# Two output projections: the merged activation's high and low parts side by side, one wide product for both, and two reads of the result

## The reference, cut to what matters

```python
# first block
merged = (gates[:, :, 0] * jnp.einsum('bsc,cd->bsd', ya, w_proj_rnn[l])
          + gates[:, :, 1] * jnp.einsum('bsc,cd->bsd', yb, w_proj_attn[l]))
x = x + jnp.einsum('bsd,de->bse', merged, w_out[l])        # output projection 1
h = rmsnorm(x, norm2_g[l])                                 # then up, gate, down
...
# second block
y = jax.nn.sigmoid(g_a) * (o_a @ w_o_swa[l]) + jax.nn.sigmoid(g_b) * (o_b @ w_o_mla[l])
x = x + y @ w_out[l]                                       # output projection 2
h = rmsnorm_2(x, ffn_norm_g[l])
x = x + (jax.nn.silu(h @ w_gate[l]) * (h @ w_up[l])) @ w_down[l]
```

## Time and profile before

| What | us |
|---|---|
| Median of 3 runs | 799.68 (799.31 to 800.32) |
| The profiled execution | 799.39 |
| Its span, first to last instruction | 797.6 |
| TensorE busy | 790.2 (99%) |
| TensorE weight loads busy | 692.8 (87%) |
| VectorE busy | 583.0 (73%) |
| ScalarE busy | 453.2 (57%) |
| GpSimd busy | 77.1 (10%) |

### The profile page before, as it was taken

How to read it: one execution, slowest core, us unless ns; L and a number is a source line. 1 busy time by engine, 2 the same in 40 slices (tenths; PEclk the granted TensorE clock), 3 DMA queues, 4 the chain that set the end, 5 groups by cost and what they waited for, 6 DMA issues and landing times.

```text
span 797.6 us, 12039 instructions
## 1 busy us (share of the span) xinstructions
PE 790.2 (99%) x4632; PEld 692.8 (87%) x4632; DVE 583.0 (73%) x706; ACT 453.2 (57%) x592; POOL 77.1 (10%) x90
## 2 busy tenths in 40 slices
PE   8999999999999999999999999999999999999997
PEld 8998888888889899999999897888799888888886
DVE  5994899566477888787877877666778766666664
ACT  7669846666435654445354758757455544454444
POOL 2330232000002100000000532410003000000000
PEclk9999999999999999999999999999999999999999
DMA  8744556434545455455454452444345555555521
GB/s 306 255 174 152 203 177 244 160 127 141 207 159 179 158 207 196 163 205 198 171 204 165 166 201 96 159 159 137 140 161 209 196 187 181 187 194 178 207 105 53
DMA packets 22582, 140.88 MB, mean 177 GB/s; under 512 B 3474, under 2 KB 3730, under 8 KB 6546
## 3 DMA queue, kind: packets, MB, share of 16 engines
q1 hardware_dynamic: 22114, 139.77, 49.2%
q10 hardware_dynamic: 432, 0.62, 0.3%
HBM read 139.33 MB, written 1.05 MB: 176 GB/s over the span
## 4 chain that ended last, share of the span: by engine, by line
PE 97%; DMA 1%; SPq 0%; DVE 0%; ACT 0%; issue 0%
PE pp L1566 21%; PE pp L1529 20%; PE pp L1531 20%; PE pp L1530 20%; PE pp L1568 10%; PE pp L1682 1%; DMA raw<-in_slabs 1%; PE pp L1708 1%; PE pp L1695 1%; PE pp L1671 1%; PE pp L1617 0%; PE pp L1745 0%; PE pp L1629 0%; PE pp L1645 0%; PE pp L1637 0%; SPq L466 0%
## 5 line engine op out<-in xcount | busy, mean ns | idle before, releaser
L946 DVE TENSOR_TENSOR wlo<-raw,whi 128x2048 fp32r<-128x2048 f32 x129 | 298.2, 2314 | 100.4 <-ACT whi L514 100.2
L514 ACT ACTIVATE whi<-raw 128x2048 fp32r<-128x2048 f32 x129 | 246.4, 1911 | 97.9 <-PE pp L1531 97.5
L1566 PE MATMUL pp<-ahilo,whi 128*128 128x512 f32 x704 | 221.4, 396 | 0.0
L1529 PE MATMUL pp<-whi,ahi 128*128 128x512 f32 (+2 forms) x412 | 163.0, 396 | 0.0
L1531 PE MATMUL pp<-whi,alo 128*128 128x512 f32 (+2 forms) x412 | 159.5, 387 | 0.0
L1568 PEld LDWEIGHTS pp<-ahilo,wlo 128*128 128x128 f32 x704 | 132.2, 188 | 31.1
L1530 PE MATMUL pp<-wlo,ahi 128*128 128x512 f32 (+2 forms) x412 | 159.2, 386 | 0.0
L1568 PE MATMUL pp<-ahilo,wlo 128*128 128x256 f32 x704 | 138.3, 278 | 0.0
L1529 PE MATMUL pp<-ahi,whi 128*128 128x256 f32 x448 | 127.8, 285 | 1.0 <-DVE wlo L1047 0.6
L1531 PE MATMUL pp<-ahi,wlo 128*128 128x256 f32 x448 | 126.7, 283 | 0.0
L1530 PE MATMUL pp<-alo,whi 128*128 128x256 f32 x448 | 126.7, 283 | 0.0
(11 more groups left out here) (230 smaller groups left out, 755.1 us busy)
## 6 DMA issues: line engine op xcount, KB each, us to landing
raw<-in_slabs SPq DMA_DIRECT2D x125, 1024.0 KB, 4.8
raw<-in_slabs SPq DMA_DIRECT2D x4, 512.0 KB, 8.3
raw<-in_slabs SPq DMA_DIRECT2D x2, 832.0 KB, 5.0
raw<-in_slabs SPq DMA_DIRECT2D x2, 576.0 KB, 3.8
raw<-in_slabs SPq DMA_DIRECT2D x4, 256.0 KB, 5.8
x_res<-in_xT SPq DMA_DIRECT2D x3, 256.0 KB, 6.4
out<-gg SPq DMA_DIRECT2D x3, 256.0 KB, 2.0
gate<-in_final_norm_g SPq DMA_DIRECT2D x1, 512.0 KB, 6.6
```

Source lines behind the costliest of these rows:

```text
L514: e.activation(whi[slot][:, :], raw[slot][:, :], ACT.Copy).then_inc(hi_ready, 1)
L946: e.tensor_tensor(wlo[slot][:, :], raw[slot][:, :], whi[slot][:, :].bitcast(f32), ALU.subtract).then_inc(lo_ready, 1)
L1529: e.matmul(out, lhs[0], rhs[0], start=first, stop=False, skip_group_check=True)
L1566: e.matmul(out[:, m, :], w[m][0], ACT2[:, k, :], start=k == 0, stop=False, skip_group_check=True)
```

## The change

The merged activation gets the side-by-side layout (`ACT0`), the projection slabs use `feature_pairs` on it, each slab writes a pair of banks (pair 1 for its first and third slab, pair 0 for its second and fourth), and VectorE adds first the left halves of both banks to the residual, then the right halves.

```diff
+def out_slab(s):
+    if S_OUT <= s < FFN1:
+        return s - S_OUT
+    return s - S2_OUT if S2_OUT <= s < FFN2 else None
@@ bank_plan
         elif s in (S2_OSWA + 1, S2_OMLA + 1):
             b = 2 + i
+        elif out_slab(s) is not None:
+            b = (3, 1)[out_slab(s) % 2]
         else:
             b = g % 2
@@ program
-        pairs = [(sb(f"ahi{i}", [P, KD, SEQ], f32r), sb(f"alo{i}", [P, KD, SEQ], f32r)) for i in range(2)]
-        ACT2 = sb("ahilo2", [P, KD, 2 * SEQ], f32r)
-        pairs.append((ACT2[:, :, 0:SEQ], ACT2[:, :, SEQ:2 * SEQ]))
+        ACT0, ACT2 = (sb(f"ahilo{i}", [P, KD, 2 * SEQ], f32r) for i in (0, 2))
+        pairs = [(ACT0[:, :, 0:SEQ], ACT0[:, :, SEQ:2 * SEQ]),
+                 (sb("ahi1", [P, KD, SEQ], f32r), sb("alo1", [P, KD, SEQ], f32r)),
+                 (ACT2[:, :, 0:SEQ], ACT2[:, :, SEQ:2 * SEQ])]
+        def out_pair(s):
+            return pp[(1, 0)[out_slab(s) % 2]]
@@ vector, residual
-                e.scalar_tensor_tensor(X[:, 2 * i:2 * i + 2, :], ps[BANK[g]][:, :].rearrange("p (m n) -> p m n", m=2),
-                                       0.5, X[:, 2 * i:2 * i + 2, :], ALU.mult, ALU.add).then_inc(bank_free["dve"], 1)
+                x = X[:, 2 * i:2 * i + 2, :]
+                link(e.scalar_tensor_tensor(x, out_pair(s)[:, :, 0:SEQ], 0.5, x, ALU.mult, ALU.add))
+                e.scalar_tensor_tensor(x, out_pair(s)[:, :, SEQ:2 * SEQ], 0.5, x, ALU.mult, ALU.add).then_inc(
+                    bank_free["dve"], 1)
@@ tensor
-            def feature_pairs(out, slot, ready):
+            def feature_pairs(out, slot, ready, act=ACT2):
...
-                        e.matmul(out[:, m, :], w[m][0], ACT2[:, k, :], start=k == 0, stop=False, skip_group_check=True)
+                        e.matmul(out[:, m, :], w[m][0], act[:, k, :], start=k == 0, stop=False, skip_group_check=True)
                     for m in range(2):
-                        ins = e.matmul(out[:, m, 0:SEQ], w[m][1], ACT2[:, k, 0:SEQ], start=False, stop=k == KD - 1,
+                        ins = e.matmul(out[:, m, 0:SEQ], w[m][1], act[:, k, 0:SEQ], start=False, stop=k == KD - 1,
...
+                    elif out_slab(s) is not None:
+                        ins = feature_pairs(out_pair(s), slot, at, ACT0)
```

## The result

| | before | after |
|---|---|---|
| median of 15 runs, us | 800.17 (799.31 to 800.44) | 801.14 (800.32 to 802.18) |
| ratio, with its 95% interval | | 1.0015 (1.0008 to 1.0022) |
| profiled span, us; granted clock | 797.6; 0.999 | 799.3; 0.999 |

The changed kernel is slower by 0.15%, 1.2 us, with an interval of 0.6 to 1.8 us (the medians themselves lie 0.97 us apart). The estimate is inside the 0.2%, 1.6 us, that the prediction called no change, though the interval reaches a little beyond it. The time is inside the range; the forecast was 800.4. The difference is real and small. Its interesting part is what it is made of.

A forecast was written before the change was run, and what follows sets the result against it. TensorE, without gaps in the projections, was taken as the bound. Block 1 at -0.42 and block 2 at +1.32 us gave +0.90, so 800.29 or 800.58 depending on the base; it took 800.4, range 798.9 to 801.8.

The forecast's parts named there:

- chunk distance: TensorE's time per projection chunk: 0.697 us, as in the feed-forward, instead of 0.7196.
- saving, projection 1: TensorE in block 1's projection: 32 chunks, each 0.0225 us shorter, save 0.72 us.
- bank wait, start of projection 2: TensorE waits until VectorE empties bank 3 of the last attention output: +1.63 us, bounds 1.1 and 1.9.
- second slab of projection 2, later than before: It waits for its weight split, queued on VectorE behind the delayed turn of chunks: starts 1.56 us later.
- F of block 2 against its P before: Block 2's first feed-forward matmul, timed from the old kernel's first projection matmul: projection 2 ends 1.02 us later.
- wait at the sum, block 1: TensorE waits for GpSimd's fold before the sum over partitions in block 1's feed-forward: +0.30 us.
- wait at the sum, block 2: The same wait for GpSimd's fold before the sum over partitions in block 2's feed-forward: +0.30 us.
- Rival 4: TensorE's gain is smaller than the feed-forward rows say, waits nearly alone: +2.0 us, 801.5; chance 0.04.
- Rival 2: No waits at all on TensorE, the pure saving of -1.44 us: 798.1; chance 0.06.
- The second pass: VectorE's second residual instruction: 0.72 us more, hidden in middle slabs; after the last, following work comes 0.90 later.
- rival 1: The bank wait alone, GpSimd's fold keeps up, for instance without residual drift of 0.18: +0.3 us, 799.8; chance 0.15.
- rival 3: At feed-forward entry GpSimd's fold collides with a VectorE pass, 2.08 instead of 1.30 us: +2.46, 802.0; chance 0.14.

The follow-up runs named there:

- run 7: The change in block 1 only; block 2 keeps the matmuls, bank and one pass of the kernel before: 800.14 against 800.16 us, ratio 0.9998.
- run 10: Changed kernel with the other bank pair in block 2 and the sum over partitions one chunk later in both blocks: 798.88 against 800.29 us before, ratio 0.9982.
- run 1: Changed kernel with projection 2's slabs writing the other bank pair, so the first avoids the pair just used: 799.74 against 800.14 us before, ratio 0.9994.
- run 5: Changed kernel with bank pairs exchanged in block 1, so its first slab writes banks still being read: 803.18 against 800.16 us before, ratio 1.0037.
- run 2: Changed kernel with ScalarE's squares ahead of `norm_hi` at each projection's last slab: 801.40 against 800.14 us before, ratio 1.0019.
- run 6: Kernel before with a second residual instruction that adds 0.0 times the bank: 800.80 against 800.16 us, ratio 1.0007.
- run 9: Changed kernel with the sum over partitions moved behind the first chunk of the first gate slab: 800.52 against 800.29 us before, ratio 1.0006.
- run 4: Changed kernel without the second residual instruction, right halves not added: 800.65 against 800.14 us before, ratio 1.0010.
- run 8: The change in block 2 only; block 1 as in the kernel before: 801.47 against 800.16 us, ratio 1.0013.
- run 3: Changed kernel with both the other bank pair in block 2 and the squares first: 799.96 against 800.14 us before, ratio 1.0000.

## Why the prediction was right, and which term was mis-sized

The comparison by steps, in us:

| step | forecast | measured |
|---|---|---|
| chunk distance | 0.697 | 0.697, (257.37 - 254.58) / 4 |
| saving, projection 1 | -0.72 | -0.72 |
| bank wait, start of projection 2 | +1.63 | +1.65 |
| second slab of projection 2, later than before | +1.56 | +1.62 |
| F of block 2 against its P before | +1.02 | +1.08 |
| wait at the sum, block 1 | +0.30 | +0.52 |
| wait at the sum, block 2 | +0.30 | +0.33 |
| sum | +0.90 | +1.21 |

**TensorE's saving.** The chunk distance came as the feed-forward rows gave it, and projection 1 has the saving in full, 0.72 us, in the changed kernel and in runs 7 and 10. In projection 2 the most that any run got is 0.59. Rival 4, that the gain is smaller, falls. The rule of the Trainium skill (TensorE: Matmul & The Clock Gate, section "Wait — 56ns, not 53.3ns?") would have given an estimated 0.32 us for both projections; 64 chunks at the measured distances give 1.44.

**The bank wait.** Where it stands, who releases it, and its size are as forecast; run 1 takes it away and run 5 makes it again elsewhere. The method was to take VectorE's quarters from before, add the restart read from the second slab, and to follow what is queued behind. The measured value lies well away from both bounds, 1.1 and 1.9. Rival 2, no waits, falls.

**The second slab.** Its start depends on the split of the weights, and that on the turn queued behind the bank wait. It came 1.62 us late, against 1.56. Run 1 shows the other half: without the bank wait the slab still waits for the weights, since TensorE is faster and VectorE is not, and so projection 2 gains 0.58 instead of 0.72. Here the prediction's starting point was wrong. It says that TensorE "waits nowhere now", but before the change the second slab waited for its weights too. This is the last matmul of the first slab, before:

```profile
589.86 0.28 PE L1531 MATMUL pp<-ahi,wlo 128*128 128x256 f32 x1
```

The next would follow 0.12 later, at 589.98, and it ran as if begun at 590.26. That is a wait of 0.28 us, and it is why projection 2 took 24.16 us and projection 1 only 23.89. In run 1 the same wait is 0.40. The error did no harm to the sum, which counts the second slab from where it really started.

**The second pass.** These are the two lines of the residual after, in the columns of the earlier trace rows:

```profile
L1219 DVE SCALAR_TENSOR_TENSOR x_res<-pp,x_res x8: 675/684/692, 240.8 to 609.6; 128x512 f32<-128x512 f32 x8
```

```profile
L1220 DVE SCALAR_TENSOR_TENSOR x_res<-pp,x_res x8: 691/691/692, 241.6 to 610.3; 128x512 f32<-128x512 f32 x8
```

The durations are 0.68 and 0.69, and in the rows the second stands 0.70 to 0.72 behind the first; 0.72 was forecast. In the middle slabs the pass hides, but only just. The third slab of block 1, to compare with the earlier trace rows:

```profile
253.20 0.69 DVE L1220 SCALAR_TENSOR_TENSOR x_res<-pp,x_res 128x512 f32<-128x512 f32 x1
254.00 2.29 DVE L961 TENSOR_TENSOR wlo<-raw,whi 128x2048 fp32r<-128x2048 f32 x1
```

```profile
252.06 1.92 ACT L529 ACTIVATE whi<-raw 128x2048 fp32r<-128x2048 f32 x1 [2.34 <-PE pp L1585]
```

The pass ends at 253.89 and `whi` at 253.98, so 0.09 us are left. At the last slab of block 1, VectorE, ScalarE and GpSimd stand as follows, to compare with the earlier trace rows:

```profile
258.06 0.68 DVE L1219 SCALAR_TENSOR_TENSOR x_res<-pp,x_res 128x512 f32<-128x512 f32 x1
258.76 0.69 DVE L1220 SCALAR_TENSOR_TENSOR x_res<-pp,x_res 128x512 f32<-128x512 f32 x1
260.11 0.48 DVE L976 SCALAR_TENSOR_TENSOR ahilo<-x_res,params,ahilo 128x256 fp32r<-128x256 f32 x1 [0.66 <-ACT ahilo L542]
260.87 0.49 DVE L976 SCALAR_TENSOR_TENSOR ahilo<-x_res,params,ahilo 128x256 fp32r<-128x256 f32 x1 [0.27 <-issue]
```

```profile
259.49 0.91 ACT L542 ACTIVATE ahilo<-x_res,params 128x256 fp32r<-128x256 f32 x2 [4.13 <-DVE x_res L1220]
260.31 0.62 ACT L546 ACTIVATE vv<-x_res 128x512 f32<-128x512 f32 x1
```

```profile
261.00 1.50 POOL L1468 TENSOR_TENSOR vv<-vv 128x512 f32<-128x512 f32 x1 [3.55 <-ACT vv L546]
262.58 0.73 POOL L1470 TENSOR_TENSOR vv<-vv 128x256 f32<-128x256 f32 x1
...
612.51 1.31 POOL L1468 TENSOR_TENSOR vv<-vv 128x512 f32<-128x512 f32 x1 [3.55 <-ACT vv L546]
613.89 0.74 POOL L1470 TENSOR_TENSOR vv<-vv 128x256 f32<-128x256 f32 x1
```

Measured from F, the fold begins at 3.63 us instead of 2.72, so 0.91 later, where 0.90 was forecast. The residuals did drift, by 0.18 to 0.19. So rival 1, that the fold keeps up, falls in both blocks. What was mis-sized is the fold's own length in block 1, which the sum put at 1.30. The prediction had said that "the last fold starts when VectorE has finished its last `lo`". In block 1 the second `lo` pass began 0.27 us after the first had ended and ran to 261.36, beyond the fold's start at 261.00, and the fold took 1.50 instead of 1.30. That is 0.20 of the 0.22 us that were missing. In block 2 both passes follow each other directly, they end at 612.51, and the fold took 1.31: there the forecast holds, 0.33 against 0.30. This looks like the mechanism of rival 3, at a quarter of its price, in one block.

Run 2 supports it from the other side, with the order reversed: the fold kept 1.30 and VectorE's pair took 2.03. The Trainium skill (SBUF — State Buffer, section "Who interferes with whom") says that a VectorE instruction with two SBUF inputs contends with a GpSimd instruction that reads SBUF, and that the order of issue decides which of them blocks. The rows of run 2 agree: 1.30 for the fold that was first, 2.03 for the pair behind it. The overlap and the 1.50 us come together in block 1 of every profile with a second pass there and the squares in their old place (runs 1, 5, 6, 7, 9 and 10 too), and both are absent in block 2, in run 4 and in block 1 of run 8. In runs 2 and 3 the fold starts first. No run removed the overlap alone, so this is a close match and not an isolated cause.

**What the local terms leave.** They sum to +1.21 us; the medians differ by 0.97 and the ratio gives 0.6 to 1.8. The profiled spans differ by 1.7. The remaining 0.45 lies before the first projection (P at 234.20 against 233.75); P of block 1 stands between 233.75 and 234.81 over the profiles of all kernels but run 5's, with no order that follows an edit; the fastest kernel, run 10, has the latest. So one profiled execution says nothing here of terms under a microsecond, unless they are read as distances inside it.

**What was luck.** The forecast of 800.4 was 0.9 us above a base of 799.5, which came from one execution and a median of three. The median of 15 of the kernel before is 800.17. The forecast is 0.74 us below the measured 801.14, and 0.67 of that is the base. That the change itself came out so close, 0.97 between the medians against 0.90, is in part chance: the local terms sum to 1.21, and the interval spans 1.2 us.

## What to carry to other kernels

When a result gets a second bank, look for the bank's previous reader before counting the matmuls saved: here the choice between two pairs at one hand-over was worth 1.65 us, more than the 1.31 that the whole change can save with both waits gone. A saving on the engine that bounds is kept only while the engines that feed it have slack at the next hand-over, so work out that slack (0.74 us here) next to the saving. Where it ran out here, moving the instruction that wants the result paid (run 9), and reordering the helpers only changed which of them was lengthened (run 2).

## What the runs showed of the hardware

- A matmul that waits for several semaphores was shown as waiting for "issue", 1.42 us, while VectorE's instruction that ended 0.11 us before it was the releaser; run 1, which takes that dependence away, removes the gap.
- Both waits of TensorE in the changed kernel cost a little more than the release. The matmul shown 0.11 us after the quarter had run as if begun 0.18 after it, and at the second slab 0.06 was shown and 0.17 effective (592.86 - 0.697 = 592.16 against 591.99).
- Where a VectorE pass that reads two operands from SBUF and a GpSimd pass over SBUF overlapped, the one that began later was the longer for it: the fold took 1.50 us instead of 1.30 (block 1 after), and the pair of `lo` passes 2.03 instead of 0.88 (run 2). No run removed the overlap alone.
- The gap of TensorE did not lower its clock. The windows of the changed kernel from the last attention matmul of block 2 over the gap, and then to F, in the columns of the earlier trace rows:

```profile
583.41:585.22 1.81, 0.39 (x3) 0.03 (x1) 1.25 (x4) 1.33 (x1) 0.00 (x0) 1.00 0.00 0
585.22:608.88 23.66, 23.53 (x137) 20.49 (x137) 20.55 (x19) 11.67 (x15) 3.83 (x2) 1.00 0.55 201
```

  TensorE works 0.39 of 1.81 us in the first, and the granted clock is 1.00, the 2.4 GHz level, in both.
- Open: why the second `lo` pass of block 1 starts 0.27 us late wherever the second residual pass is there, and never in block 2. The profile says "issue", which may hide a wait for several semaphores here too.
